# Four weight tiles of two phases loaded one stage earlier, and the pads cleared inside the next phase

## The reference

```python
def first_block(x, mem, ...):
    u = rms_norm(x, norm_mix_g[l]) @ w_in[l]
    y_ssd = ssd_mixer(u[..., :SSD_IN], ...)
    y_rwkv = rwkv7_mixer(u[..., SSD_IN:], ...)
    x = x + jnp.concatenate([y_ssd, y_rwkv], axis=-1) @ w_out[l]
    h, m = rms_norm(x, norm_x_g[l]), rms_norm(mem, norm_mem_g[l])
    x = x + memory_cross_attention(h, m, wq, wk, wv, wo)
    h = rms_norm(x, norm_ffn_g[l])
    x = x + jnp.square(jax.nn.relu(h @ ffn_w1[l])) @ ffn_w2[l]
```

## Time and profile before

| | us |
|---|---|
| median of 3 runs | 2967.31 |
| lowest and highest of them | 2962.93, 2968.71 |
| span of the profiled execution | 2966.1 |
| PE busy in it | 2842.9 (96%) |
| DVE, ACT, POOL busy | 1836.1, 1236.0, 383.0 |

### The profile page before, as it was taken

How to read it: one execution, slowest core, us unless ns; L and a number is a source line. 1 busy time by engine, 2 the same in 40 slices (tenths; PEclk the granted TensorE clock), 3 DMA queues, 4 the chain that set the end, 5 groups by cost and what they waited for, 6 DMA issues and landing times. The chain is left out here.

```text
span 2966.1 us, 60381 instructions
## 1 busy us (share of the span) xinstructions
PE 2842.9 (96%) x24198; PEld 2790.0 (94%) x24198; DVE 1836.1 (62%) x2183; ACT 1236.0 (42%) x1485; POOL 383.0 (13%) x501
## 2 busy tenths in 40 slices
PE   8999587999997999999999999999999999999997
PEld 8998486899997999999999999999999999999997
DVE  6657744777543565655555676798657655765664
ACT  5343211354333444343434454534454443444443
POOL 0000121020001015810182120000110000010011
PEclk9999788999999999999999999999999999999999
DMA  6663000456651656676566655545555665556564
GB/s 230 193 195 128 15 1 1 143 199 197 195 188 62 196 188 199 192 237 195 187 197 196 230 193 168 207 171 185 172 198 183 199 195 191 196 194 194 184 200 141
DMA packets 138270, 514.02 MB, mean 173 GB/s; under 512 B 15345, under 2 KB 15601, under 8 KB 136817
## 3 DMA queue, kind: packets, MB, share of 16 engines
q1 hardware_dynamic: 138096, 511.58, 52.7%
HBM read 503.12 MB, written 8.40 MB: 172 GB/s over the span
## 5 line engine op out<-in xcount | busy, mean ns | idle before, releaser
L656 PE MATMUL acc<-a,hi 128*128 128x256 f32 x5504 | 1526.8, 277 | 23.1 <-DVE lo L463 21.2
L657 PE MATMUL acc<-a,hi 128*128 128x256 f32 x5504 | 1521.4, 276 | 0.0
L658 PE MATMUL acc<-a,lo 128*128 128x256 f32 x5504 | 1521.3, 276 | 0.0
L463 DVE TENSOR_TENSOR lo<-raw,hi 128x1024 fp32r<-128x1024 f32 x704 | 897.7, 1291 | 678.1 <-ACT hi L371 676.5
L656 PEld LDWEIGHTS acc<-a,hi 128*128 128x128 f32 x5504 | 1035.1, 188 | 27.3 <-issue 21.6
L657 PEld LDWEIGHTS acc<-a,hi 128*128 128x128 f32 x5504 | 1035.2, 188 | 0.8 <-issue 0.5
L658 PEld LDWEIGHTS acc<-a,lo 128*128 128x128 f32 x5504 | 1035.2, 188 | 0.0
L371 ACT ACTIVATE hi<-raw 128x1024 fp32r<-128x1024 f32 x704 | 734.1, 1057 | 649.1 <-PE acc L658 627.2
L608 POOL TENSOR_TENSOR a<-th,a 128x512 f32 (+1 forms) x64 | 84.9, 1327 | 1381.2 <-ACT a L416 1381.1
L463 DVE TENSOR_TENSOR lo_x<-raw_x,hi_x 128x1024 fp32r<-128x1024 f32 x128 | 162.3, 1281 | 117.5 <-ACT hi_x L371 117.5
L656 PE MATMUL acc<-a,hi_in 128*128 128x256 f32 x768 | 213.7, 278 | 10.2 <-DVE lo_in L463 10.2
(11 more groups left out here) (476 smaller groups left out, 2869.9 us busy)
## 6 DMA issues: line engine op xcount, KB each, us to landing
raw<-in_ffn SPq DMA_DIRECT2D x256, 512.0 KB, 4.2
raw_in<-in_w_in SPq DMA_DIRECT2D x96, 512.0 KB, 4.2
raw<-in_w_in SPq DMA_DIRECT2D x92, 512.0 KB, 3.6
raw<-in_up_gate SPq DMA_DIRECT2D x88, 512.0 KB, 4.4
raw<-in_up_val SPq DMA_DIRECT2D x88, 512.0 KB, 4.4
raw<-in_down SPq DMA_DIRECT2D x88, 512.0 KB, 4.2
raw_x<-in_wq SPq DMA_DIRECT2D x32, 512.0 KB, 4.4
raw_x<-in_wk SPq DMA_DIRECT2D x32, 512.0 KB, 4.3
```

Of the source, the lines that this page charges most:

```text
L463: eng.tensor_tensor(self.lo[:, slot, :], self.raw[:, slot, :], self.hi[:, slot, :].bitcast(F32), ALU.subtract).then_inc(self.s_lo, 1)
L656: eng.matmul(out, self.hi[:, slot, cols], a[:, 0, :], start=opens, stop=False)
L657: eng.matmul(out, self.hi[:, slot, cols], a[:, 1, :], start=False, stop=False)
L658: ins = eng.matmul(out, self.lo[:, slot, cols], a[:, 0, :], start=False, stop=closes)
```

## The change

`wr` gets its first four chunks loaded in the block of `rwkv_output`, and `fo` its first four in the block of `cross_attention`. For the first, `rwkv_output` lays out `next_raw` at the address that `raw` has in the ring of the next stage (`room` in front of it makes up the distance; the buffers that stood there were used up to the end of `rwkv_chunks` and are given back ahead of it). For the second, the tiles go into `qx`, once the eight groups of scores are done, and `qx` becomes the `raw` of the ring of `feed_forwards`. Behind that, SP leaves these chunks out (`skip=RING`). The block `clear_pads` is gone: DVE clears `tb` behind the splits of the first unit of `fo`, and ACT does the small exponential behind its splits of that unit.

```diff
-    def prefetch(self, eng, ph):
+    def prefetch(self, eng, ph, raw):
+
+        eng.wait_ge(self.s_lo, ph.base["c"])
         for c in range(RING):
-            self.load(eng, ph, c, c)
+            slot = (ph.base["c"] + c) % RING
+            eng.dma_start(raw[:, slot, :], ph.w[c + ph.w0]).then_inc(self.s_raw[slot], 16)
...
-def rwkv_output(nc, s, u, b, low, lw):
+def rwkv_output(nc, s, u, b, low, lw, wr):
...
+        room = alloc(nc, st, "next_room", [P, (NEXT_RING - U_TILES * T - 2 * 1024 - 16 * (Q + 1) - 2 * RW * T)])
+        raw = alloc(nc, st, "next_raw", [P, RING, CK * UNIT])
...
+            @block.sync
+            def _(eng):
+                s.prefetch(eng, wr, raw)
...
+    raw = qx[:].rearrange("p (r a) t -> p r (a t)", r=RING)
     with nc.Block() as block:
+        @block.sync
+        def _(eng):
+            eng.wait_ge(scd, 8)
+            s.prefetch(eng, fo, raw)
...
-                        s.sp(eng, wr)
+                        s.sp(eng, wr, skip=RING)
...
-def clear_pads(nc, s):
-    with nc.Block() as block:
-        @block.vector
-        def _(eng):
-            eng.memset(s.tb[:], 0.0)
...
-        clear_pads(nc, s)
+        cleared = sem("pads_cleared")
+
+        def steps(eng, v):
+            if v == 0:
+                tables.act_steps(eng)
+
+        def clear_pads(eng, v):
+            if v == 0:
+                eng.memset(s.tb[:], 0.0).then_inc(cleared, 1)
+                eng.wait_ge(cleared, 1)
...
-                    s.sp(eng, ph)
+                    s.sp(eng, ph, skip=RING if ph is fo else 0)
...
-                tables.act_steps(eng)
-                s.act(eng, ffn + [pa], aside=tables.act_waves, at=ffn[1], finish=False)
+                s.act(eng, ffn + [pa], aside=tables.act_waves, at=ffn[1], finish=False, beside=(fo, steps))
...
-                s.dve(eng, ffn, aside=tables.dve_inverse, at=ffn[1], finish=False)
+                s.dve(eng, ffn, aside=tables.dve_inverse, at=ffn[1], finish=False, beside=(fo, clear_pads))
```

More of the change, by code:

```diff
@@ L57 @@
 XH, XD = 4, 512
+NEXT_RING = 21504
 Q2, K2, V2, S2, GA2, GS2 = 0, 8, 9, 10, 14, 30
@@ L252, in gain, with ring @@
         return g[:, i:i + 1] if isinstance(i, int) else g[:, bass.ds(i, 1)]
-    def ring(self, stack, tag, parts=True):
+    def ring(self, stack, tag, parts=True, raw=None):
         nc = self.nc
@@ L259, in sb @@
             return stack.enter_context(nc.sbuf_tensor(name + tag, shape, dt))
+        place = sb("raw", [P, RING, CK * UNIT])
+        self.raw = place if raw is None else raw
         room = sb("ring_room", [P, (PART_AT - ACT_AT) // 4])
-        self.raw = sb("raw", [P, RING, CK * UNIT])
         self.hi = sb("hi", [P, RING, CK * UNIT], F32R)
@@ L1242, in _ @@
                                       s.a0[:, RW + 4 * h:RW + 4 * h + 4, 0, :].bitcast(F32), ALU.subtract)
+    return raw
 def rwkv(nc, dram, s, u, low, lw):
+    wr = s.phase("w_out_r", "w_out_r", 8, 2, 2, s.a0[:, 8:16], "acc")
     with ExitStack() as st:
         b = {n: alloc(nc, st, n, shape) for n, shape in (
[L1248 to L1253, removed]
+            ("f1", [P, 2 * RW, Q + 1]), ("kk", [P, RW, T]), ("bb", [P, RW, T]))}
+        with ExitStack() as early:
+            b.update({n: alloc(nc, early, n, shape) for n, shape in (
+                ("kr", [P, RW, NCH, 2, Q]), ("vt", [P, NCH, 1024]), ("bt", [P, 1024]), ("kt", [P, 1024]),
+                ("sfac", [P, RW]), ("xpk", [P, 16 * 32]), ("zpk", [P, 16 * 32]))})
+            rwkv_prepare(nc, dram, s, u, b, low, lw)
+            rwkv_chunks(nc, dram, s, u, b, low, lw)
+        raw = rwkv_output(nc, s, u, b, low, lw, wr)
+    return wr, raw
 class ChunkedScan:
@@ L1576, in pool, with cross_attention @@
         eng.tensor_tensor(self.sq[:, 0, :], self.sq[:, 0, :], self.sq[:, 1, :], ALU.add).then_inc(self.added, 1)
-def cross_attention(nc, s, qx, kx, vx, pe_, pt, stats, a1, sem):
+def cross_attention(nc, s, qx, kx, vx, pe_, pt, stats, a1, sem, fo):
     scale = XD ** -0.5
@@ L1670, in _, with attentions @@
             s.pe(eng, phs)
-def attentions(nc, dram, s, u):
+def attentions(nc, dram, s, u, wr, raw):
     with ExitStack() as st:
         sem = semaphores(nc, st)
-        wr = s.phase("w_out_r", "w_out_r", 8, 2, 2, s.a0[:, 8:16], "acc")
         with ExitStack() as early:
@@ L1686, in attentions @@
                 room = alloc(nc, rg, "scan_room", [P, 2 * LINE])
-                s.ring(rg, "_x")
+                s.ring(rg, "_x", raw=raw)
+                assert 4 * NEXT_RING == 4 * (KT * 2 * T + 3 * KT * T + 2 * LINE)
                 ws = s.phase("w_out_s", "w_out_s", 8, 2, 4, s.a0, "gained", out=a1, g="norm_x_g",
@@ L1731, in attentions @@
                 stats = alloc(nc, xs, "stats", [P, 16])
-                cross_attention(nc, s, qx, kx, vx, pe_, pt, stats, a1, semaphores(nc, xs))
-    return a1
+                fo = s.phase("wo", "wo", 8, 4, 2, a1, "gained", out=s.a0, g="norm_ffn_g")
+                cross_attention(nc, s, qx, kx, vx, pe_, pt, stats, a1, semaphores(nc, xs), fo)
+    return a1, fo, qx[:].rearrange("p (r a) t -> p r (a t)", r=RING)
 def final_norm(nc, s, g, out_dram=None):
@@ L2391, in dve, with feed_forwards @@
             one()
-def feed_forwards(nc, dram, s, a1, out_dram, states):
+def feed_forwards(nc, dram, s, a1, fo, raw, out_dram, states):
     with ExitStack() as st:
@@ L2397, in feed_forwards @@
         ub = alloc(nc, st, "ub", [P, 2 * KT, T])
-        s.ring(st, "_2")
+        s.ring(st, "_2", raw=raw)
         with ExitStack() as early:
@@ L2410, in feed_forwards @@
         a2 = alloc(nc, st, "a2", [P, KT, 2, T], F32R)
-        fo = s.phase("wo", "wo", 8, 4, 2, a1, "gained", out=s.a0, g="norm_ffn_g")
         ffn = [fo]
@@ L2544, in build @@
         s_zero = whole.enter_context(nc.semaphore("pads_zeroed"))
-        u = mixers(nc, dram, s, s_load, s_prm, s_const, s_zero)
+        u, wr, raw = mixers(nc, dram, s, s_load, s_prm, s_const, s_zero)
         states = nc.dram_tensor("state_tables", (4, P, S5_COLS), F32, kind="Internal").ap()
-        a1 = attentions(nc, dram, s, u)
-        feed_forwards(nc, dram, s, a1, out_dram, states)
+        a1, fo, raw = attentions(nc, dram, s, u, wr, raw)
+        feed_forwards(nc, dram, s, a1, fo, raw, out_dram, states)
 def alloc(nc, stack, name, shape, dt=F32):
@@ L2613, in _ @@
                     s.pe(eng, phs)
-        rwkv(nc, dram, s, u, low, lw)
-    return u
+        wr, raw = rwkv(nc, dram, s, u, low, lw)
+    return u, wr, raw
 def tiled(a):
```

## The result

The changed kernel takes 2954.97 us (median of 6 runs, 2952.25 to 2961.85), the kernel before beside it 2966.7 us (6 runs). The ratio is 0.9967 with a 95% interval of 0.9957 to 0.9977, that is 6.8 to 12.8 us less. The forecast was 2958.6 us and a range of 2954.0 to 2963.5. The profiled span went from 2966.1 to 2954.5 us.

What follows compares the result with a forecast made beforehand. PE, busy for 96% of the span, was taken to bound the kernel. 6.5 us before `fo` plus 2.2 at the start of `wr` made 8.7, from the median 2967.31 to 2958.6 us; range 2954.0 to 2963.5.

Steps and rivals of the forecast that it cites:

- the sum: Whole kernel: 6.5 us before `fo` plus 2.2 at the start of `wr`, 8.7 us gained; chance 0.55.
- The pause before `fo`: Between `cross_attention` and `fo`: PE starts at 952.66 instead of 959.14, taking 6.5 us from the path.
- the 5 us of half clock behind the pause: Start of `fo`: the same 5 us at half clock kept; bounds 2.4 us more gain or 2 us less.
- The split of it: Pause before `fo`: 1.2 us from the memset's block, 5.3 from the exponential, two small loads and the load.
- No new wait: Start of `fo`: moved memset costs nothing, 0.93 us without cover; exponential leaves POOL 3 us idle; fifth chunk does not stall.
- The start of `wr`: Block of `wr`: PE gains its 1.28 us wait, later splits come 2.6 earlier; 2.2 us taken, bounds 0.7 and 2.6.
- The step that failed: Between the start of `wr` and `cross_attention`: no further gain counted; moving as a whole was stated only behind `fo`.
- (a): Before `fo`: the clock does not fall in the shorter pause; gain 11.1 us, 2956.2 us; chance 0.17.
- (b): Start of `wr`: only 0.7 us there, the clock rising when it does now; gain 7.2, 2960.1 us; chance 0.12.
- (c): Opening of `feed_forwards`: an engine's code fetch stalls some 2 us; gain 6.7, 2960.6 us; chance 0.06.
- (d): Both places: half clock goes on, 20 us more at both makes it 10.1 us slower, 2977.4 us; chance 0.02.
- (e): Both places: loads come too late to matter, only the memset's block goes; gain 1.2 us, 2966.1 us; chance 0.05.

Runs made afterwards that it cites:

- `fo` alone: Against the kernel before, only the first four tiles of `fo` loaded early; memset block, exponential ahead of the splits and `wr` as before: 2961.15 us, ratio 0.9973.
- The two runs with PE at full clock: Changed kernel with matmuls added around the pause before `fo` and behind `rwkv_output`: 6, 11 and 30 took 2964.1 us; 2, 5 and 15 took 2954.59 us.

## Where the prediction was right, and where not

The time lay in the range, near its lower end, and the direction was right. The change's own part is 10.3 us, where the sum had 8.7: 0.2 more in the pause, 0.5 more at the start of `wr`, and 0.9 at a place that the sum did not have.

- **The pause before `fo`, 6.5 us: measured 6.73.** Every step held: ACT at once, then 1.09 and 1.37 us. The 0.2 is the opening of the block: 1.40 us behind DVE's last step, where I had taken the 1.69 to DVE's memset. That the 5 us of half clock behind the pause stayed was an assumption, and in part luck: in the second profile of the changed kernel they were 4.6, in that with `fo` alone 3.5.
- **The split of it, 1.2 for the block and 5.3 for the rest:** measured alone, the early load with the exponential still ahead gave 5.2, and the block 1.5 (2.25 with a faster landing).
- **No new wait:** right for the memset (though without cover it would have cost 0.08 us and not 0.93), the exponential (4.0 us of POOL's idle time left, 3 forecast) and the fifth chunk.
- **The start of `wr`, 2.2 us: 2.7** (2.45 at the product with `da`, 2.66 at the third chunk). The reasoning held as to its limits: the clock rose 5.3 us behind PE's start and not 8.8, and the third chunk's low part is what limits then, at 2.6 by the prediction. The two runs with PE at full clock showed the same limit. The term should have been that limit, not the 2.2.
- **The step that failed** is the silent assumption that all between the start of `wr` and `cross_attention` moves as a whole, as the prediction said for what lies behind `fo`. Behind `fo` it held in the two profiles. Between the two places it did not: 0.9 us more came at the next place where the clock changes. The prediction put that at nothing; its bounds and rivals had the clock change only at the two places themselves.
- **The rivals.** (a) did not come: the clock fell in the pause in all five profiles with a pause of 5.3 to 5.4 us and no added matmuls. (b), 0.7 us at the start of `wr`, was refuted by the 2.7. (c) was refuted by the kernel with `fo` alone. (d) did not come in the changed kernel, but half clock did go on when the low part was made late: 6.9 us more of it behind PE's start in the block of `wr` than in the changed kernel. (e) is refuted: the early tiles give 8.8 of the 10.3 us.
- The Trainium skill ("TensorE: Matmul & The Clock Gate", Part 1) says that the number of slow matmuls at a start varies from run to run of the same kernel and isn't worth fitting a model to. The profiles agree: the slow part at the start of `fo` was 5.1 us in one profile of the changed kernel and 4.6 in the other, and 3.5 to 5.2 over the nine profiles without added matmuls. At 0.47 us for each us of half clock that is a difference of up to 0.8 us.
- The Trainium skill ("Runtime: NRT & Kernel Launch", Instruction fetch mechanics) says that a taken branch to code that is not yet fetched stalls. That did not show at the start of the block of `feed_forwards`. In the changed kernel DVE's first step comes 1.17 us and PE's 2.54 us after the block opens, which could hide a short stall; but with the memset first DVE started 0.30 us after the opening (950.68), and with added matmuls PE started 0.05 us after it (945.24).

## What to carry to other kernels

Where a stage without loads stands ahead of one that begins with a load, read the chain load, split, multiply from the timeline: the engines' own steps remain, and all that stands ahead of the first of them can go. One tile, early enough, gave the whole gain here; the other three could land while PE worked on the first, at half clock. A small step in a block of its own costs the meeting of the engines, not its own time: the memset cost 1.5 us with its block and at most 0.1 without.

## What was not expected of the hardware

- The clock's falls and rises follow the program closely: near 598 the length of a half-speed stretch depended in 13 of 13 profiles on whether PE restarted ahead of the fall or behind it, by 1.5 us or less. A gain can in this way bring another microsecond, or lose one, at a later place.
- Filling a pause with matmuls is no safe way to hold the clock: with 1.42 us left open before `fo` it stayed at 1.00, with 1.93 it fell there, and the filling then ran at half clock itself; ahead of `wr` it stayed at 1.00 with 2.19 us open. The length of the gap alone does not decide it.
- A float32 matmul of 256 columns on plain float32 operands ran as two instructions of about 0.22 us, where one of the stream's takes 0.11.
- A load of 512 KB behind two small ones was there 3.70, 4.26, 4.32 and 4.47 us after its issue in four profiles (up to the start of the split that waits for it).
